# Small f32 matmuls on halves and quarters of the array in a woven single-core kernel

## The chip, the cores and the metric

One core of a Trainium2 chip runs the whole program. The metric is the device time of one execution in microseconds; the median of several runs is compared.

## The reference

Two blocks of a language model are applied to 256 tokens of 2048 columns, in f32. The first block has two layers. In each, one projection feeds four groups of eight heads of 64 columns: retention, hgrn2, mlstm and rwkv7. Their outputs are joined and projected, and a gated feed-forward part follows. The second block has two attentions. What matters here, cut:

```python
# retention, in chunks; mlstm has the same shape, with its own decay, and a denominator
scores = jnp.einsum('bhtd,bhsd->bhts', qc, kc) * intra
out = jnp.einsum('bhts,bhse->bhte', scores, vc) + ...
# rwkv7, token by token
state = (state * jnp.exp(lwt)[:, :, None, :]
         - jnp.einsum('bhvk,bhk->bhv', state, kkt)[..., None] * (at * kkt)[:, :, None, :]
         + vt[..., None] * kt[:, :, None, :])
y = jnp.einsum('bhvk,bhk->bhv', state, rt)
# second block, first attention: three branches per head (compressed, selected, window)
o = g[..., 0:1] * o_cmp + g[..., 1:2] * o_sel + g[..., 2:3] * o_win
```

## The kernel before

The program is a series of stages, each a block in which every engine has its own instruction list and waits for the others by semaphores. The large products are split into a high and a low part of the weights: SP loads slabs of weights into a ring of four, ACT writes the high part (line 183), DVE or POOL the low part (line 191), and PE multiplies both with two parts of the activations. Between the stages of the mixers this work is woven in: `Woven` cuts the next projection into pieces (a quarter of a pair of output tiles and of its rows), and `weave.pe(pe, step)` issues as many pieces as the shares for that step say (lines 510 to 512, three matmuls for each 128 rows: 12 matmuls in a piece of a 2048-row matrix, 9 in the w_out piece of 1536 rows). In these stages POOL writes the low part, and two slabs (eight pieces) fit beside each other.

The rwkv group works in chunks of 64 tokens. A chunk needs the inverse of a triangular matrix, and `rwkv_solve_stage` builds it from products of matrices. A pass j takes two heads (hh) and two tiles of 128 tokens (tt), four matrices x. Each is 128x128 with its two 64x64 chunk blocks on the diagonal, and zeros elsewhere. The pass has ten steps: step 1 multiplies keys (64 rows deep) into four masked matrices; steps 2 to 7 square, multiply and add them; steps 8 to 10 apply three of them to the right-hand sides z. Every step is a burst of matmuls on PE (lines 1803 and after, all through the helper `mats`), then an evacuation from PSUM by DVE (lines 1884 to 1909), which PE awaits. `RWKV_SHARES` puts two woven pieces behind step 1, one behind steps 2, 3, 5 and 6, none behind the others.

`rwkv_output_stage` computes, per pass, masked products (line 2007) and then for each head and token tile two value products and two state products (lines 2018 to 2022).

`retention_stage` and `mlstm_stage` go head by head: `decayed_product` (lines 1100, 1101; 64 rows deep), woven pieces (four and three), then for the head before `weighted_values` (lines 1109, 1110; its output has 64 columns of the array), in mlstm twice, the second time with ones. DVE weights the products between the two (lines 1192 and 1351).

`attention_stage` goes by units of two heads and one query tile, with one or two key tiles: scores (lines 2592, 2595), soft-max on DVE and ACT, transposes (2610, 2614), value products (2625), with 3, 2 and 1 woven pieces between them in the first attention.

On PE one f32 matmul of the program is two instructions in the trace.

Of the kernel before, what the change touches and what calls it, by code (L numbers as in the profile page):

```python
# [13 lines left out]
P = 128  # L14
# [729 lines left out]
def constants():  # L744
# [48 lines left out]
    c["low8"] = chunk & b8 & (u < s)  # L793
    c["up8"] = chunk & b8 & (u > s)
    c["low_off"] = chunk & ~b8 & (u < s)
    c["up_strict"] = chunk & (u > s)
# [300 lines left out]
def decayed_product(pe, m, h, k, q, out):  # L1097

    j, r = h // 2, slice(HD * (h % 2), HD * (h % 2) + HD)
    m.nc.tensor.matmul(out[:, 0:T], k[r, j, 0:P], q[r, j, :], start=True, stop=True)  # L1100
    return m.nc.tensor.matmul(out[:, T:T + P], k[r, j, P:T], q[r, j, P:T], start=True, stop=True)


def weighted_values(pe, m, h, v, w, out, first=True):

    r = slice(HD * (h % 2), HD * (h % 2) + HD)
    m.nc.tensor.matmul(out[r, 0:T], v(0), w[:, 0:T], start=first, stop=False)
    return m.nc.tensor.matmul(out[r, P:T], v(1), w[:, T:T + P], start=False, stop=True)  # L1110
# [10 lines left out]
def retention_stage(m, p, weave):  # L1121
# [13 lines left out]
    with nc.Block() as block:  # L1135
        @block.sync
        def _(sp):
            tables.start(sp, cs, m.const_dram("ret_cos_sin"))
            tables.start(sp, decay, m.const_dram("ret_decay").rearrange("p (h n) -> p h n", h=NH))
            weave.sp(sp, NH + 1)  # L1140

        @block.tensor
        def _(pe):
# [7 lines left out]
            for h in range(NH + 1):  # L1151
                if h < NH:
                    if h >= 2:

                        pe.wait_ge(*weights.at(h - 1))
                    decayed_product(pe, m, h, k, q, m.ps[:, 2 + h % 2, :]).then_inc(*scores.up())
                    weave.pe(pe, 1 + h)
                if h >= 1:
                    g_ = h - 1
                    pe.wait_ge(*weights.at(h))  # L1160
                    weighted_values(pe, m, g_, lambda st: vt[:, st, g_ * HD:(g_ + 1) * HD], pr[:, g_ % 2, :],
                                    m.ps[:, g_ // 4, (g_ // 2 % 2) * T:(g_ // 2 % 2) * T + T]).then_inc(*o_done.up())
            weave.pe(pe, NH + 1)

        @block.gpsimd
        def _(pool):
            weave.pool(pool, NH + 1)

        @block.scalar
        def _(act):  # L1170
# [3 lines left out]
            weave.act(act, NH)  # L1174
            act.wait_ge(*o_done.at(NH))
            nc.scalar.activation(q, m.banks(0, 2).rearrange("p (a b) -> p a b", b=T), ACT.Copy)
            weave.act(act, NH + 1)

        @block.vector
        def _(dve):  # L1180
# [7 lines left out]
            for h in range(NH):  # L1188
                dve.wait_ge(*scores.at(h + 1))
                if h >= 2:  # L1190
                    dve.wait_ge(*o_done.at(h - 1))
                nc.vector.tensor_tensor(pr[:, h % 2, :], m.ps[:, 2 + h % 2, 0:384], decay[:, h, :], ALU.mult)\
                    .then_inc(*weights.up())
# [10 lines left out]
def mlstm_stage(m, par, gates, weave):  # L1204
# [26 lines left out]
    with nc.Block() as block:  # L1231
        @block.sync
        def _(sp):
            moved.start(sp, log_f, m.tmp[NH:2 * NH, 1, 0, :])
            tables.start(sp, mask, m.const_dram("mlstm_mask"))
            weave.sp(sp, NH + 3)

        @block.tensor
        def _(pe):
# [24 lines left out]
            for h in range(NH + 1):  # L1264
                if h < NH:
                    if h >= 2:
                        pe.wait_ge(*weights.at(h - 1))
                    decayed_product(pe, m, h, k, q, m.ps[:, 4 + h % 2, :]).then_inc(*scores.up())
                    weave.pe(pe, 3 + h)
                if h >= 1:  # L1270
                    g = h - 1

                    pe.wait_ge(*weights.at(h))
                    half = (g // 2 % 2) * T
                    weighted_values(pe, m, g, lambda st: vt[:, st, g * HD:(g + 1) * HD], pr[:, g % 2, :],
                                    m.ps[:, g // 4, half:half + T])
                    weighted_values(pe, m, g, lambda st: ones[:, 0:HD], pr[:, g % 2, :],
                                    m.ps[:, 2 + g // 4, half:half + T]).then_inc(*o_done.up())
            weave.pe(pe, NH + 3)

        @block.gpsimd
        def _(pool):
            weave.pool(pool, NH + 3)

        @block.scalar
        def _(act):
# [13 lines left out]
            weave.act(act, NH + 2)  # L1300
            act.wait_ge(*o_done.at(NH))
            nc.scalar.activation(acc[:, 0:GT, :], m.banks(2, 2).rearrange("p (a b) -> p a b", b=T), ACT.Abs).then_inc(*den_ready.up())
            weave.act(act, NH + 3)

        @block.vector
        def _(dve):
# [40 lines left out]
            for h in range(NH):  # L1347
                dve.wait_ge(*scores.at(h + 1))
                if h >= 2:
                    dve.wait_ge(*o_done.at(h - 1))  # L1350
                nc.vector.tensor_tensor(pr[:, h % 2, :], m.ps[:, 4 + h % 2, 0:384], ex[:, h, :], ALU.mult)\
                    .then_inc(*weights.up())
            dve.wait_ge(*o_done.at(NH))
# [390 lines left out]
def mask4(ap):  # L1744

    return ap.unsqueeze(1).unsqueeze(1).broadcast_to([P, 2, 2, P])
# [5 lines left out]
def rwkv_solve_stage(m, weave):  # L1752
# [8 lines left out]
    masks = m.flat(S_AT, 6 * P).rearrange("p (a b) -> p a b", b=P)  # L1761
# [9 lines left out]
    x1 = m.tmp[:, 0, 2:4, :].rearrange("p a (x n) -> p (a x) n", n=P)  # L1771
# [9 lines left out]
    with nc.Block() as block:  # L1781
        @block.sync
        def _(sp):
            for n, name in enumerate(("low8", "up8", "low_off", "up_strict", "up_incl", "up_incl_neg")):
# [1133 lines left out]
```

## Time and profile before

| | |
|---|---|
| median of 3 runs | 4463.32 us |
| lowest, highest | 4458.55, 4469.31 us |
| the profiled execution | 4464.4 us, span 4462.1 us |
| mean granted TensorE clock | 0.934 |
| PE busy | 3881.6 us (87%) |
| DVE, ACT, POOL busy | 2094.1, 1695.6, 1647.4 us (47, 38, 37%) |

The page gives the busy time of every engine over the span; PE is a matmul engine whose ends are modelled, so that its busy time says little of its pace. The timeline lists instructions in order of time and merges equal ones that follow each other; the brackets give the idle time of the engine before them and what ended it. A granted clock of 1.00 is 2.4 GHz, 0.50 is 1.2 GHz.

### The profile page before, as it was taken

Reading aid. Unit: us, or ns where it says so; the run is one execution under the profiler, and the core shown is the slowest. Engines: PE = TensorE matmul, PEld = TensorE weight load, DVE = VectorE, ACT = ScalarE, POOL = GpSimd, SP = SyncE. Lnnn points to the kernel's source line nnn. Section 1 sums busy time; section 2 is a strip of 40 time slices with the busy share of each in tenths; the row PEclk is TensorE's granted clock in tenths of the full one; section 3 lists DMA queues with packets and bytes.
Section 4 is the critical chain, followed back from the end, with each engine's and each line's share of the span. In section 5 each row is a group of like instructions: output and inputs, shape, how many; then the busy total and the mean of one; then the engine's idle time right before and its main releaser. Section 6 shows DMA issues by size and latency. Waiting matters only on the chain. (4 is left out here: it accounts for less than half of the span.)

```text
span 4462.1 us, 58395 instructions
## 1 busy us (share of the span) xinstructions
PE 3881.6 (87%) x24692; PEld 3426.4 (77%) x24692; DVE 2094.1 (47%) x2118; ACT 1695.6 (38%) x1540; POOL 1647.4 (37%) x649
## 2 busy tenths in 40 slices
PE   6787888889999997887888979999996978989987
PEld 6676877778888886776777868888885877878776
DVE  4534543455454555633643255554455432344454
ACT  3402433344443443411543334444343324544433
POOL 0322555379992000321554449994000024440000
PEclk9898998999999998998899989999998979999998
DMA  4411333367775553411333447776552633335443
GB/s 159 132 48 55 102 122 116 130 201 232 237 237 166 184 184 126 136 52 43 104 106 116 165 137 239 238 241 197 160 180 95 203 111 98 114 107 180 162 149 113
DMA packets 379713, 655.58 MB, mean 147 GB/s; under 512 B 13792, under 2 KB 191856, under 8 KB 378384
## 3 DMA queue, kind: packets, MB, share of 16 engines
q1 hardware_dynamic: 364624, 598.50, 41.9%
q0 software_dynamic: 14912, 54.53, 3.6%
q8 instruction: 134, 2.20, 0.2%
q14 instruction: 43, 0.35, 0.0%
HBM read 645.63 MB, written 6.29 MB: 146 GB/s over the span
## 5 line engine op out<-in xcount | busy, mean ns | idle before, releaser
L212 PE MATMUL ps<-x_parts,w_hi 128*128 128x512 f32 x6160 | 2199.0, 401 | 172.5 <-ACTq L397 114.3
L213 PE MATMUL ps<-x_parts,w_lo 128*128 128x256 f32 x6160 | 1741.2, 283 | 0.0
L183 ACT ACTIVATE w_hi<-weight_ring 128x2048 fp32r<-128x2048 f32 (+1 forms) x564 | 1065.7, 1890 | 1723.7 <-PE ps L213 1125.0
L212 PEld LDWEIGHTS ps<-x_parts,w_hi 128*128 128x128 f32 x6160 | 1170.9, 190 | 470.9 <-issue 108.5
L191 DVE TENSOR_TENSOR w_lo<-weight_ring,w_hi 128x2048 fp32r<-128x2048 f32 x392 | 952.6, 2430 | 1113.8 <-ACT w_hi L183 1113.8
L191 POOL TENSOR_TENSOR w_lo<-weight_ring,w_hi 128x2048 fp32r<-128x2048 f32 (+1 forms) x172 | 790.3, 4598 | 1691.5 <-ACT w_hi L183 1691.5
L213 PEld LDWEIGHTS ps<-x_parts,w_lo 128*128 128x128 f32 x6160 | 1179.7, 192 | 0.0
L510 PE MATMUL ps<-x_parts,w_hi 128*128 128x256 f32 x2592 | 792.3, 306 | 130.4 <-POOL w_lo L191 67.2
L511 PE MATMUL ps<-x_parts,w_hi 128*128 128x256 f32 x2592 | 754.7, 291 | 0.0
L512 PE MATMUL ps<-x_parts,w_lo 128*128 128x256 f32 x2592 | 752.8, 290 | 0.0
L510 PEld LDWEIGHTS ps<-x_parts,w_hi 128*128 128x128 f32 x2592 | 518.7, 200 | 163.1 <-POOL w_lo L191 83.0
L511 PEld LDWEIGHTS ps<-x_parts,w_hi 128*128 128x128 f32 x2592 | 519.4, 200 | 3.9 <-issue 2.9
L512 PEld LDWEIGHTS ps<-x_parts,w_lo 128*128 128x128 f32 x2592 | 518.1, 200 | 0.0
L2310 POOL TENSOR_SCALAR spare<-spare,second_vectors 128x512 f32<-128x512 f32 x180 | 403.1, 2247 | 3.9
L2314 POOL TENSOR_TENSOR arena<-arena,spare 128x512 f32<-128x512 f32 x180 | 350.5, 1947 | 14.6
L1803 PE MATMUL ps<-arena 128*128 128x128 f32 (+2 forms) x1024 | 133.1, 297 | 38.5 <-DVE arena L1909 18.1
L113 POOL DMA_DIRECT2D arena<-in_w_ck x2 | 1.8, 909 | 436.8 <-DVE w_lo L191 436.8
L1803 PEld LDWEIGHTS ps<-arena 128*128 128x128 f32 (+1 forms) x1024 | 117.8, 205 | 51.4 <-DVE arena L1909 22.8
L113 POOL DMA_DIRECT2D spare<-in_w_ada x96 | 72.9, 759 | 178.2 <-POOLq L983 150.9
L1004 PE MATMUL ps<-arena,small_consts 128*128 128x256 f32 x256 | 76.7, 469 | 49.9 <-ACT arena L991 49.9
L1004 PEld LDWEIGHTS ps<-arena,small_consts 128*128 128x128 f32 x256 | 60.7, 242 | 65.6 <-ACT arena L991 54.4
L2683 DVE SCALAR_TENSOR_TENSOR arena<-ps,arena 128x256 f32<-128x256 f32 (+1 forms) x40 | 20.5, 553 | 176.8 <-PE ps L2595 139.9
(386 smaller groups left out, 2769.2 us busy)
## 6 DMA issues: line engine op xcount, KB each, us to landing
weight_ring<-in_w_in SPq DMA_DIRECT2D x212, 1024.0 KB, 5.2
weight_ring<-in_w_ffn_gate SPq DMA_DIRECT2D x88, 1024.0 KB, 5.3
weight_ring<-in_w_ffn_up SPq DMA_DIRECT2D x88, 1024.0 KB, 5.4
weight_ring<-in_w_ffn_down SPq DMA_DIRECT2D x88, 1024.0 KB, 5.6
spare<-in_w_ada POOLq DMA_DIRECT2D x96, 512.0 KB, 5.2
weight_ring<-in_w_out SPq DMA_DIRECT2D x32, 768.0 KB, 4.6
weight_ring<-in_w_out SPq DMA_DIRECT2D x24, 1024.0 KB, 5.1
weight_ring<-in_w_br_a SPq DMA_DIRECT2D x8, 1024.0 KB, 5.0
```

The lines of the kernel that those rows point to most:

```text
L113: eng.dma_start(dst, src).then_inc(self.rec[0], 16)
L183: core.nc.scalar.activation(core.w_hi[:, g % 2, at], core.ring[:, (self.start + g) % RING, at], ACT.Copy)\
L191: (ops or core.nc.vector).tensor_tensor(core.w_lo[:, g % 2, at], core.ring[:, (self.start + g) % RING, at], core.w_hi[:, g % 2, at].bitcas ...
L212: mm(out, hi, core.x_parts[:, x, :, :].rearrange("p a t -> p (a t)"), start=first, stop=False)
L213: return mm(out[:, 0:T], lo, core.x_hi[:, x, :], start=False, stop=last)
L510: mm(out, hi, x_hi, start=(kk == 0), stop=False)
L511: mm(out, hi, x_lo, start=False, stop=False)
L512: last = mm(out, lo, x_hi, start=False, stop=(kk == 2 * self.ks - 1))
L1004: mm = nc.tensor.matmul(m.ps[:, n, 0:T], m.const("ones"), sq[:, k, :], start=(k == 0), stop=(k == KT - 1))
L1803: return nc.tensor.matmul(at, lhs, right, start=True, stop=True)
L2310: ins = nc.gpsimd.tensor_scalar(to, buf[:, n % 2, k, :], c[:, 2 * s + k:2 * s + k + 1], None, ALU.mult)
L2314: done(pool, nc.gpsimd.tensor_tensor(out, out, buf[:, n % 2, k, :], ALU.add), step)
```

## The change

In the solve all chunk matrices are kept compact: 128 partitions (two chunks of 64) by 64 columns, four matrices in 256 columns of an array or a PSUM bank. A product of two of them is two matmuls of 64x64 on 64 columns, one in the quarter of rows and columns 0 to 63, one in that of 64 to 127. The masks are cut to 64 columns, and the unit matrix is the stacked one. Step 1 computes each chunk block by itself, in all four quarters. The right-hand sides keep their 512 columns. Retention and mlstm go by pairs of heads, whose matmuls alternate between the two row halves or column halves, and their woven pieces come in steps of 8 and 6. The output stage does the same, token tile by token tile. The first attention issues the value products alternately for its two column halves, and both attentions issue the scores in the order 0, 2, 1, 3.

```diff
-    c["low8"] = chunk & b8 & (u < s)
...
+        return np.take_along_axis(x, i[:, None] // CHUNK * CHUNK + np.arange(CHUNK)[None, :], 1)
+    c["low8"] = own_chunk(b8 & (u < s))
...
+def decayed_products(pe, m, j, k, q, bank):
+    for hh, r in by_halves():
+        m.nc.tensor.matmul(m.ps[:, bank + hh, 0:T], k[r, j, 0:P], q[r, j, :], start=True, stop=True)
+    for hh, r in by_halves():
+        mm = m.nc.tensor.matmul(m.ps[:, bank + hh, T:T + P], k[r, j, P:T], q[r, j, P:T], start=True, stop=True)
+    return mm
+def weighted_values(pe, m, v, w, out):
+    for hh, r in by_halves():
+        m.nc.tensor.matmul(out[r, 0:T], v(hh, 0), w[:, hh, 0:T], start=True, stop=False)
+    for hh, r in by_halves():
+        mm = m.nc.tensor.matmul(out[r, P:T], v(hh, 1), w[:, hh, T:T + P], start=False, stop=True)
+    return mm
...
+            for j in range(GT + 1):
+                if j < GT:
+                    if j:
+                        pe.wait_ge(*weights.at(2 * j))
+                    decayed_products(pe, m, j, k, q, 2).then_inc(*scores.up())
+                if j:
+                    n = j - 1
+                    pe.wait_ge(*weights.at(2 * j))
+                    weighted_values(pe, m, lambda hh, st: vt[:, st, (2 * n + hh) * HD:(2 * n + hh + 1) * HD], pr,
+                                    m.ps[:, n // 2, n % 2 * T:n % 2 * T + T]).then_inc(*o_done.up())
+                if j < GT:
+                    weave.pe(pe, 1 + j)
...
-        return m.flat(t0, 512).rearrange("p (x n) -> p x n", n=P)
+        return m.flat(t0, 4 * CHUNK).rearrange("p (x n) -> p x n", n=CHUNK)
...
-            def mats(bank, lhs, right, x, out=None):
-                at = m.ps[:, bank, x * P:(x + 1) * P] if out is None else out
-                return nc.tensor.matmul(at, lhs, right, start=True, stop=True)
+            def mats(out, lhs, right):
+                for r in chunk_rows():
+                    mm = nc.tensor.matmul(out[r], lhs[r], right[r], start=True, stop=True)
+                return mm
...
-                        for hh in range(2):
-                            r = slice(HD * hh, HD * hh + HD)
-                            mm = mats(0, l[r, j, tk], rr[r, j, tk], 2 * hh + tt, m.ps[:, bank + 3 * hh, tk])
+                        for hh, r in by_halves():
+                            for c, out_rows in enumerate(chunk_rows()):
+                                tk = slice(tt * P + c * CHUNK, tt * P + c * CHUNK + CHUNK)
+                                mm = nc.tensor.matmul(m.ps[out_rows, bank + 3 * hh, tt * CHUNK:(tt + 1) * CHUNK],
+                                                      l[r, j, tk], rr[r, j, tk], start=True, stop=True)
...
-            ps = [m.ps[:, b, :].rearrange("p (x n) -> p x n", n=P) for b in range(3)]
+            ps = [m.ps[:, b, 0:4 * CHUNK].rearrange("p (x n) -> p x n", n=CHUNK) for b in range(3)]
...
+                for tt in range(2):
+                    at = j % 2 * T + tt * P
...
+                    for hh in range(2):
+                        nc.tensor.matmul(outs[hh][:, at:at + P], vt[:, tt, heads[hh]], low[:, 0, 2 * hh + tt, :], start=True, stop=False)
...
-MLSTM_SHARES = ([6, 2, 7] + [3] * NH + [2], [2, 64])
-RETENTION_SHARES = ([8] + [4] * NH + [3], [3, 64])
+MLSTM_SHARES = ([6, 2, 7] + [6] * GT + [2], [2, 64])
+RETENTION_SHARES = ([8] + [8] * GT + [3], [3, 64])
...
-                for x, (q, keys, bank) in enumerate(items):
+                for x in (0, 2, 1, 3):
+                    q, keys, bank = items[x]
...
+                order = [(n, o) for n in range(size) for o in range(len(outs))] if cmp is not None else \
+                    [(n, o) for o in range(len(outs)) for n in range(size)]
```

Two places of PE's list show how the instructions move. The first is the start of a pass of the solve (L1803 is `mats` before; L1826 is `mats` and L1842 the products of step 1 after). Before:

```order
L1803 MATMUL ps<-arena 128x128 x4
L1803 MATMUL ps<-arena 128x2x64 x12
L1803 MATMUL ps<-arena 128x128 x12
L510 MATMUL ps<-x_parts,w_hi 128x256
L511 MATMUL ps<-x_parts,w_hi 128x256
L512 MATMUL ps<-x_parts,w_lo 128x256
```

After:

```order
L1826 MATMUL ps<-arena 64x64 x8
L1826 MATMUL ps<-arena 64x2x64 x24
L1842 MATMUL ps<-arena 64x64 x24
L510 MATMUL ps<-x_parts,w_hi 128x256
L511 MATMUL ps<-x_parts,w_hi 128x256
L512 MATMUL ps<-x_parts,w_lo 128x256
```

These rows are step 7 (four products), steps 8 to 10 (twelve) and step 1 of the next pass (twelve). Every product has become two, each on a quarter; what stands between them has not moved.

The second place is the mlstm stage, between two woven stretches. Before, the values and the ones of one head and the products of a later one:

```order
L1109 MATMUL ps<-arena 64x256
L1110 MATMUL ps<-arena 64x128
L1109 MATMUL ps<-arena,small_consts 64x256
L1110 MATMUL ps<-arena,small_consts 64x128
L1100 MATMUL ps<-arena 128x256
L1101 MATMUL ps<-arena 128x128
L510 MATMUL ps<-x_parts,w_hi 128x256
```

After, twice as many of each for a pair of heads, the products first (L1109 and L1111 are now `decayed_products`, L1118 and L1120 `weighted_values`):

```order
L1109 MATMUL ps<-arena 128x256 x2
L1111 MATMUL ps<-arena 128x128 x2
L1118 MATMUL ps<-arena 64x256 x2
L1120 MATMUL ps<-arena 64x128 x2
L1118 MATMUL ps<-arena,small_consts 64x256 x2
L1120 MATMUL ps<-arena,small_consts 64x128 x2
L510 MATMUL ps<-x_parts,w_hi 128x256
```

The bursts of two heads have come together, and the woven stretches between them have grown from three pieces to six.

## Rows read from the trace of the kernel before

**Rows 1.** The page: the weight splitting groups of part 5.

```profile
L183 ACT ACTIVATE w_hi<-weight_ring 128x2048 fp32r<-128x2048 f32 (+1 forms) x564 | 1065.7, 1890 | 1723.7 <-PE ps L213 1125.0
...
L191 POOL TENSOR_TENSOR w_lo<-weight_ring,w_hi 128x2048 fp32r<-128x2048 f32 (+1 forms) x172 | 790.3, 4598 | 1691.5 <-ACT w_hi L183 1691.5
```

**Rows 2.** Timeline of PE, solve, layer 0, first pass: start, length, what ran, [idle].

```profile
214.90 1.61 PE L1803 MATMUL ps<-arena 64*128 64x128 f32 x24
...
219.42 2.79 PE L1803 MATMUL ps<-arena 128*128 128x128 f32 x24
...
223.92 2.05 PE L1803 MATMUL ps<-arena 128*128 128x128 f32 x16 [0.23 <-DVE tmp L1892]
...
227.42 1.16 PE L1803 MATMUL ps<-tmp,arena 128*128 128x128 f32 x8
...
234.35 2.05 PE L1803 MATMUL ps<-arena 128*128 128x128 f32 x16 [0.55 <-DVE arena L1901]
...
239.86 1.16 PE L1803 MATMUL ps<-arena 128*128 128x128 f32 x8 [0.85 <-DVE arena L1906]
```

**Rows 3.** Timeline of DVE in the same pass.

```profile
216.65 2.48 DVE L1884 TENSOR_TENSOR arena<-ps,arena 128x512 f32<-128x512 f32 x4 [17.17 <-PE ps L1803]
...
223.45 0.42 DVE L1892 COPY tmp<-ps 128x256 f32<-128x256 f32 x1
...
228.68 0.69 DVE L1897 TENSOR_TENSOR arena<-tmp,ps 128x512 f32<-128x512 f32 x1 [1.32 <-PE ps L1803]
```

**Rows 4.** Windows: us; busy (x) of PE, PEld, DVE, ACT, POOL; PEclk; DMA; GB/s.

```profile
214.90:345.30 130.40, 110.15 (x865) 102.08 (x864) 51.58 (x84) 13.81 (x13) 27.22 (x6) 0.93 0.16 49
1911.45:2038.90 127.45, 107.49 (x865) 99.61 (x864) 51.62 (x84) 13.81 (x13) 27.22 (x6) 0.96 0.16 50
1984.44:2015.34 30.90, 25.91 (x218) 24.01 (x218) 12.90 (x21) 2.56 (x3) 8.43 (x2) 1.00 0.22 69
216.65:250.42 33.77, 28.77 (x217) 26.57 (x217) 12.91 (x21) 4.09 (x3) 9.07 (x2) 0.88 0.20 63
245.00:250.00 5.00, 4.15 (x32) 3.86 (x30) 0.69 (x1) 0.00 (x0) 0.00 (x0) 0.50 0.69 210
350.00:395.00 45.00, 39.87 (x408) 33.69 (x407) 13.65 (x24) 6.80 (x7) 9.03 (x2) 0.96 0.08 24
```

**Rows 5.** Timeline of PE, output stage, layer 0.

```profile
352.45 0.68 PE L1981 MATMUL ps<-arena 64*64 64x64 f32 x16
...
362.08 1.56 PE L1992 MATMUL ps<-arena,tmp 64*64 64x64 f32 x64
...
369.35 0.43 PE L2018 MATMUL ps<-arena 128*64 128x128 f32 x2
...
369.93 0.44 PE L2022 MATMUL ps<-arena 64*64 64x64 f32 x4
370.30 0.43 PE L2018 MATMUL ps<-arena 128*64 128x128 f32 x2
```

**Rows 6.** Timeline of PE, mlstm stage, layer 0.

```profile
633.30 0.65 PE L1109 MATMUL ps<-arena 128*64 128x256 f32 x2
...
634.00 0.59 PE L1109 MATMUL ps<-arena,small_consts 128*64 128x256 f32 x2
...
634.74 0.70 PE L1100 MATMUL ps<-arena 64*128 64x256 f32 x2
...
635.59 0.39 PE L510 MATMUL ps<-x_parts,w_hi 128*128 128x256 f32 x1
```

**Rows 7.** Timeline of PE, hgrn stage, layer 0.

```profile
484.35 0.87 PE L1453 MATMUL ps<-arena,h 128*64 128x256 f32 x8
```

**Rows 8.** Timeline of PE, first attention of the second block.

```profile
3709.93 0.72 PE L2592 MATMUL ps<-arena 64*128 64x128 f32 x8
...
3719.29 1.09 PE L2625 MATMUL ps<-arena 128*64 128x128 f32 x8
...
3722.04 0.39 PE L510 MATMUL ps<-x_parts,w_hi 128*128 128x256 f32 x1
```

More of the change, by code:

```diff
@@ L1094, in head_norm_stage, with by_halves @@
     m.end()
[L1097 to L1110, printed above, removed]
+def by_halves():
+    return [(hh, slice(HD * hh, HD * hh + HD)) for hh in range(2)]
+def decayed_products(pe, m, j, k, q, bank):
[10 more added lines that the diff above has]
+    return mm
 def transpose_values(pe, m, v, bank):
@@ L1150, in _ @@
             pe.wait_ge(*v_ready.at(1))
[L1151 to L1163, printed above, removed]
+            for j in range(GT + 1):
[10 more added lines that the diff above has]
+                    weave.pe(pe, 1 + j)
+            weave.pe(pe, GT + 1)
         @block.gpsimd
         def _(pool):
-            weave.pool(pool, NH + 1)
+            weave.pool(pool, GT + 1)
         @block.scalar
@@ L1187, in _ @@
             nc.vector.tensor_tensor(qk, qk, rot, ALU.add).then_inc(*qk_ready.up())
[L1188 to L1193, printed above, removed]
+            for j in range(GT):
+                dve.wait_ge(*scores.at(j + 1))
+                if j:
+                    dve.wait_ge(*o_done.at(j))
+                for hh in range(2):
+                    nc.vector.tensor_tensor(pr[:, hh, :], m.ps[:, 2 + hh, 0:384], decay[:, 2 * j + hh, :], ALU.mult)\
+                        .then_inc(*weights.up())
     m.end()
@@ L1346, in _ @@
             done(dve, nc.vector.tensor_tensor(ex, ex, bcast(mask, NH), ALU.mult), masked)
[L1347 to L1353, printed above, removed]
+            for j in range(GT):
+                dve.wait_ge(*scores.at(j + 1))
+                if j:
+                    dve.wait_ge(*o_done.at(j))
+                for hh in range(2):
+                    nc.vector.tensor_tensor(pr[:, hh, :], m.ps[:, 4 + hh, 0:384], ex[:, 2 * j + hh, :], ALU.mult)\
+                        .then_inc(*weights.up())
+            dve.wait_ge(*o_done.at(GT))
             dve.wait_ge(*least.at(1))
@@ L1744, in mask4, with chunk_rows @@
 def mask4(ap):
-    return ap.unsqueeze(1).unsqueeze(1).broadcast_to([P, 2, 2, P])
+    return ap.unsqueeze(1).unsqueeze(1).broadcast_to([P, 2, 2, ap.shape[-1]])
+def chunk_rows():
+    return [slice(CHUNK * c, CHUNK * c + CHUNK) for c in range(2)]
 SOLVE_STEPS = 1 + 10 * GT
@@ L1783, in _ @@
         def _(sp):
-            for n, name in enumerate(("low8", "up8", "low_off", "up_strict", "up_incl", "up_incl_neg")):
+            for n, name in enumerate(("low8", "up8", "low_off", "up_strict")):
                 tables.start(sp, masks[:, n, :], m.const_dram(name))
+            for n, name in enumerate(("up_incl", "up_incl_neg")):
+                tables.start(sp, incl[:, 4 + n, :], m.const_dram(name))
             weave.sp(sp, SOLVE_STEPS - 1)
```

126 lines of the change are left out of this document (65 added, 61 removed).

## The prediction

> **What bounds the kernel now.** I read the page first, then the timeline of PE and of DVE in each stage that the diff touches. The profiled execution took 4464.4 us, 1.1 us above the median of the runs, 4463.32; the sums below are made against 4464.4. PE is the engine to watch. Everywhere in the touched stages it alternates bursts of small f32 matmuls with woven pieces (12 matmuls of the next projection in a stage that weaves a 2048-row matrix), and it stands still only for evacuations.
>
> In the solve one pass over two heads is a chain of ten steps: a burst, DVE's evacuation, and a woven piece that covers the evacuation where there is one. From start to start the first pass has 4.52 us for step 1 (214.90 to 219.42), 4.50 for step 2, 3.50 for step 3, 6.93 for steps 4 and 5, 5.51 for steps 6 and 7 (of which 2.01 step 7, as step 4: a burst of 1.16 and 0.85 of idle time) [rows 2]. An undisturbed pass, at a granted clock of 1.00, takes 30.90 us [rows 4], so steps 8 to 10 take 5.94. A burst of 24 instructions (an f32 matmul is two instructions) lasts 2.79 us, one of 16 2.05, one of 8 1.16 [rows 2]. Where no piece covers it, the evacuation costs 0.85 us of PE's idle time [rows 2]: 0.10 until DVE starts, 0.69 for 512 columns (227.42 + 1.16 = 228.58, DVE at 228.68 [rows 3]), 0.06 back. The first pass of layer 0 took 33.77 us at a mean clock of 0.88: in its window of 245 to 250 the clock stood at 0.50, the 1.2 GHz level, after bursts of 8 with idle time between them. The two solve stages take 130.40 and 127.45 us at 0.93 and 0.96 [rows 4], 258 together, 10 more than 8 x 30.90.
>
> **The price of a small matmul.** This is the number that everything hangs on.
> - One quarter of the array, one after the other: 4 instructions of 64x64 on 64 columns, 0.44 us. Two diagonal quarters in turn: 16 instructions, 0.68 us [rows 5]. Four more pairs cost 0.24 us, so a pair is a slot of 0.06 us, and two quarters of different rows and columns do work at once. A burst of 8 slots is 0.68, 16 slots 1.16, 24 slots 1.64.
> - The 64 instructions of L1992 last 1.56 us [rows 5], 0.024 each, so at times more than two quarters run together. That is the cheap end (a 24-slot burst at 1.2 us). The dear end is one quarter at a time, 0.06 for each instruction, 2.8 us for the same burst.
> - I take the 0.06 per pair, since L1981 goes through the same two diagonal quarters as the new solve.
> - Two column halves in turn: the hgrn stage runs 8 instructions (4 on 256, 4 on 128 columns) in 0.87 us [rows 7], while 4 such instructions on one half take 0.70 from start to start [rows 6]. So the second half is nearly free.
>
> **The solve.** Step 1 becomes 48 instructions in four quarters. Twelve slots give 0.92 instead of 1.61, and what follows the burst (4.52 - 1.61 = 2.91) stays: 3.83. Step 3 (and 6, which has the same form, 5.51 - 2.01 = 3.50): 16 slots and 1.45 of woven piece beyond the burst (3.50 - 2.05), 2.61 each. Step 2: 1.64 + 1.45 = 3.09. The evacuations shrink from 512 to 256 columns, 0.42 for a single one [rows 3] and about 0.37 in a row, so the pieces of steps 2, 3 and 6 hide them whole; the 0.23 and 0.55 of idle time that stand there now [rows 2] go, which I left in the 1.45 for the entry into the burst. Steps 4 and 7 have no piece: 0.68 + 0.10 + 0.42 + 0.06 = 1.26. Step 5 is late on DVE, since its third copy keeps 512 columns: 1.64 + 0.10 + 0.37 + 0.37 + 0.69 + 0.06 = 3.23. Steps 8 to 10 keep their 512-column evacuation: 0.68 + 0.85 = 1.53 each, 4.59. The pass is 3.83 + 3.09 + 2.61 + 1.26 + 3.23 + 2.61 + 1.26 + 4.59 = 22.5 us, 8.4 less, 67 for the eight. The four mask products of step 1 (2.48 us on DVE now [rows 3], some 1.5 then) lie beside two woven pieces before and after: nothing. So do the smaller mask tables.
>
> Against it stands the clock. Steps 7 to 10 are now 4.6 of 8.0 us busy; they will be 2.7 of 5.9. I expect six of eight passes to fall to the 1.2 GHz level there, and each to pay 4.5 us, more than the 2.9 us (33.77 - 30.90) of the pass above, because the bursts that carried the recovery are shorter. That is 26 us where 10 are paid now: 16 lost. The solve gives **51 us**.
>
> **The output stage.** For each head and token tile PE now spends 0.95 us (369.35 to 370.30) [rows 5], all on its path; in future the two heads of a pair go through the same sequence on opposite halves. Two saved per pair of heads, 0.95 x 2 x 4 x 2 layers = **15 us**.
>
> **Mlstm and retention.** Per head: 0.70 for the values, 0.74 for the sums with ones, 0.85 for the products [rows 6], 2.29 in all, and 1.55 in retention, which has no ones. Pairs pay it once: 2.29 x 4 x 2 = 18.3 and 1.55 x 4 x 2 = 12.4. DVE's weighting is covered by 6 or 8 pieces instead of 3 or 4. What comes due is the supply. A slab of weights needs 1.89 us on ACT and 4.60 on POOL [rows 1] after its buffer comes free, some 6.8 us with the hand-overs, and its predecessor holds PE 5.8 us (four pieces of 1.45). Now each mlstm slab has a head's work between its pieces. With pairs two slabs per layer have none, and the one after each waits 1.0 us: 4 us off the 18.3. Retention's slabs have three quarters of the rows and its pair work falls on every second slab boundary, so they do not wait. **14 + 12 us**.
>
> **Attention.** The value products of a unit with both key tiles run 10 instructions on one half of the columns, then 10 on the other, 2.75 us (3719.29 to 3722.04) [rows 8]. Taken in turn they need half, 1.37 less; units with one key tile have 12 instructions in place of 20, 0.82 less. Eight of each: 17.5, of which I leave 1 to the supply: **16.5 us**. The new order of the scores is worth nothing: 8 instructions of 64 rows on 128 columns last 0.72 us [rows 8], where 24 of them in strict turn last 1.61 [rows 2]; (1.61 - 0.72) / 16 = 0.056 each, half of the 0.11 of a full-height one, and eight of those in a single file would need over 0.9. The two row halves already overlap across such a short distance.
>
> The sum is 51 + 15 + 14 + 12 + 16.5 = 109: 4464.4 - 109 = 4355, or **4354** on the median's scale.
>
> **The rule that speaks against the change.** In the solve the two diagonal quarters write one PSUM bank, each its own 64 partitions; L1981 and L1992 [rows 5] write a bank for each row half, and no row of this trace shows two row halves writing one bank at once. The Trainium skill ("TensorEngine Tiling (Array Packing)", Restrictions and Gotchas, Gotcha 1) says that different row tiles cannot access the same PSUM bank simultaneously. By that rule the time is rival A's.
>
> **The rivals.**
> - A, one bank, one quarter at a time. A pair costs 0.12 instead of 0.06. Each pass has 120 such slots (all but step 1), 7.0 us, 56 for eight; the output stage loses 4. PE stays busier, so the clock's extra 16 is not paid. 109 - 56 - 4 + 16 = 65: **4398**. For it: no row to the contrary. Against it: the partitions differ, and column halves write one bank together without loss [rows 7].
> - B, the supply takes over. POOL's 4.60 and ACT's 1.89 [rows 1] decide in mlstm, retention and attention, and the 43 us there come to nothing: 109 - 43 = 66, **4397**. Against it: POOL is idle 1691 us for ACT, and ACT waits for PE [rows 1], so in most places PE is the late one.
> - C, slower: the clock stays at the 1.2 GHz level through both solves and output stages, as it was in the window of 245 to 250 [rows 4]. The solves keep PE busy for 110 and 107 us, less the 67 saved, and an output stage for 40 [rows 4], less 8: 215 us in all. Doubled, less the 26 already counted, they cost 189: **4543**. It decides against the change from 109 us of extra low-clock cost. Against it: the clock came back within the stages each time, and their means are 0.93 and 0.96 [rows 4].
>
> **How the numbers follow.** My forecast 0.78, A 0.12, B 0.06, C 0.03, and 0.01 for gains and losses that cancel. Differences under 0.2% (9 us) are about what a measurement of this kernel can't tell from none. Faster by more: 0.96; within: 0.01; slower: 0.03. With quarters at the cheap end (18 us more), no fall of the clock at all (26 more) and no waits for supply (5) the time would be 4305; all three together are unlikely, so the range begins at 4318. It ends at 4402, above A and B.
>
> **What would show it.** Bursts of the solve at 1.6, 1.2 and 0.7 us (A: 2.8, 2.0, 1.1); passes of 22.5 us where the clock stays up and some 27 where it falls; the clock low at the end of six of eight passes; an output stage of 1.9 us per pair of heads instead of 3.8; one value and one product burst per pair in mlstm and retention; value products of 1.4 us in attention, scores unchanged at 0.72. I am wrong if diagonal pairs take 0.12 us, if "PE waits for POOL" grows by tens of us, or if the woven matmuls of the solve run mostly at the low clock.

## The result, and the profile after

The changed kernel takes 4352.91 us (median of 4 runs, 4351.05 to 4353.90), beside 4466.32 for the kernel before: a ratio of 0.9748, 95% interval 0.9731 to 0.9765. Its profiled execution took 4353.9 us, span 4351.6, mean clock 0.932; against the execution of before (4464.4) that is 110.5 us less, where 109 were forecast.

The page of the kernel after: busy time of PE, and of the groups that answer to [rows 1].

```profile
PE 3769.8 (87%) x25844; PEld 3333.2 (77%) x25844; DVE 2056.8 (47%) x2118; ACT 1695.3 (39%) x1540; POOL 1645.1 (38%) x649
...
L191 POOL TENSOR_TENSOR w_lo<-weight_ring,w_hi 128x2048 fp32r<-128x2048 f32 (+1 forms) x172 | 790.8, 4602 | 1581.7 <-ACT w_hi L183 1581.6
...
L510 PE MATMUL ps<-x_parts,w_hi 128*128 128x256 f32 x2592 | 790.3, 305 | 140.5 <-POOL w_lo L191 76.4
```

PE lost 112 us of busy time. POOL's split costs the same as before, 4.6 us a slab. The woven matmuls of L510 wait 76.4 us for low parts; before it was 67.2.

**The solve.** The timeline of PE in the first pass of layer 0, as in [rows 2]; the helper `mats` is now L1826, step 1 L1842:

```profile
214.23 0.93 PE L1842 MATMUL ps<-arena 64*64 64x64 f32 x48
...
218.15 1.61 PE L1826 MATMUL ps<-arena 64*64 64x64 f32 x48
...
221.33 1.15 PE L1826 MATMUL ps<-arena 64*64 64x64 f32 x32
...
224.03 0.68 PE L1826 MATMUL ps<-tmp,arena 64*64 64x64 f32 x16
...
225.31 0.45 PE L1826 MATMUL ps<-arena 64*64 64x64 f32 x8 [0.59 <-DVE arena L1925]
225.59 0.39 PE L1826 MATMUL ps<-tmp,arena 64*64 64x128 f32 x4
...
228.88 1.15 PE L1826 MATMUL ps<-arena 64*64 64x64 f32 x32
...
231.59 0.68 PE L1826 MATMUL ps<-arena 64*64 64x64 f32 x16
232.86 1.09 PE L1826 MATMUL ps<-arena 64*64 64x128 f32 x16 [0.59 <-DVE arena L1934]
...
236.69 1.09 PE L1826 MATMUL ps<-arena 64*64 64x128 f32 x16 [0.86 <-DVE arena L1937]
238.64 0.93 PE L1842 MATMUL ps<-arena 64*64 64x64 f32 x48 [0.86 <-DVE arena L1937]
```

From start to start the steps take 3.92, 3.18, 2.70, 1.28, 3.57, 2.71, 1.27, and 1.88, 1.95, 1.95 us (between 236.69 and 238.64 lies step 10). The bursts of 8, 16 and 24 slots last 0.68, 1.15 and 1.61 us. But steps 8 to 10 show 1.09 us bursts of the form 64x128, and step 5 runs the same form between its 64x64 instructions. DVE in the same pass, as in [rows 3]:

```profile
215.32 1.42 DVE L1912 TENSOR_TENSOR arena<-ps,arena 128x256 f32<-128x256 f32 x4 [15.68 <-PE ps L1842]
...
228.05 0.68 DVE L1929 COPY arena<-ps 128x512 f32<-128x512 f32 x1
...
232.38 0.42 DVE L1934 COPY arena<-ps 128x256 f32<-128x256 f32 x1 [1.48 <-PE ps L1826]
```

The windows that answer to [rows 4]: both solve stages, one pass, a stretch of steps 8 to 10, and the 30 us behind the first solve.

```profile
214.23:312.21 97.98, 82.88 (x1441) 74.45 (x1440) 35.62 (x84) 13.82 (x13) 27.30 (x6) 1.00 0.22 66
1862.43:1960.04 97.61, 82.88 (x1441) 74.45 (x1440) 35.62 (x84) 13.82 (x13) 27.28 (x6) 1.00 0.22 66
214.23:238.64 24.41, 20.72 (x361) 18.61 (x360) 8.91 (x21) 4.48 (x4) 9.08 (x2) 1.00 0.14 45
234.00:239.00 5.00, 2.54 (x55) 2.06 (x59) 2.06 (x3) 0.00 (x0) 4.19 (x1) 1.00 0.01 3
312.00:342.00 30.00, 25.48 (x380) 23.72 (x380) 11.64 (x23) 5.01 (x4) 8.05 (x2) 0.83 0.12 37
```

The stages take 97.98 and 97.61 us instead of 130.44 and 127.41 (from the first burst to the end of DVE's last instruction): 32.5 and 29.8 less, **62 us**. All four passes of each run at a clock of 1.00, also where PE is busy for 2.54 of 5 us. In layer 0 it falls right behind the stage (0.83 over the next 30 us); in layer 1 it stays at 1.00 there for another 6 us.

**Output stage, mlstm, attention**, the timelines that answer to [rows 5, 6, 8]:

```profile
339.09 0.44 PE L2045 MATMUL ps<-arena 128*64 128x128 f32 x4
...
340.06 0.44 PE L2045 MATMUL ps<-arena 128*64 128x128 f32 x4
...
341.02 1.16 PE L2035 MATMUL ps<-arena 64*128 64x128 f32 x16
```

One head pair and tile takes 0.97 us, so a pair of heads 1.93 instead of 3.8.

```profile
597.07 0.70 PE L1109 MATMUL ps<-arena 64*128 64x256 f32 x4
...
597.92 0.65 PE L1118 MATMUL ps<-arena 128*64 128x256 f32 x4
...
598.62 0.60 PE L1118 MATMUL ps<-arena,small_consts 128*64 128x256 f32 x4
...
599.37 0.39 PE L510 MATMUL ps<-x_parts,w_hi 128*128 128x256 f32 x1
```

Both heads of a pair go through products, values and sums in 2.30 us (597.07 to 599.37), as one head did before.

```profile
3612.39 1.09 PE L2661 MATMUL ps<-arena 128*64 128x128 f32 x16
...
3613.78 0.39 PE L510 MATMUL ps<-x_parts,w_hi 128*128 128x256 f32 x1
```

The value products of a unit with two key tiles take 1.39 us (3612.39 to 3613.78), not 2.75.

### The profile page after: what moved, and what is told of

Read it like the earlier page. It is cut to its first block and busy times, and to the rows that moved or that the text cites. A ratio compares the mean times of both kernels' runs of the same rounds, so it can differ in the third digit from the quotient of the medians.

```text
span 4351.6 us, 60687 instructions
## 1 busy us (share of the span) xinstructions
PE 3769.8 (87%) x25844; PEld 3333.2 (77%) x25844; DVE 2056.8 (47%) x2118; ACT 1695.3 (39%) x1540; POOL 1645.1 (38%) x649
## 5 line engine op out<-in xcount | busy, mean ns | idle before, releaser
L510 PE MATMUL ps<-x_parts,w_hi 128*128 128x256 f32 x2592 | 790.3, 305 | 140.5 <-POOL w_lo L191 76.4
L510 PEld LDWEIGHTS ps<-x_parts,w_hi 128*128 128x128 f32 x2592 | 518.3, 200 | 175.1 <-POOL w_lo L191 93.5
L311 ACT ACTIVATE tmp<-ps 128x1024 f32<-128x1024 f32 x86 | 85.1, 990 | 42.0 <-PE ps L213 42.0
L1826 PE MATMUL ps<-arena 64*64 64x64 f32 (+1 forms) x1664 | 76.0, 234 | 23.1 <-DVE arena L1937 13.2
```

The lines of the kernel that those rows point to most:

```text
L311: nc.scalar.activation(tmp, core.ps[:, CB * par:CB * par + n, T:2 * T], ACT.Copy).then_inc(core.cross_copied.sem, 1)
L510: mm(out, hi, x_hi, start=(kk == 0), stop=False)
L1826: mm = nc.tensor.matmul(out[r], lhs[r], right[r], start=True, stop=True)
```

## The experiments

### Each part put back by itself

Four kernels, each the changed one with one part as in the kernel before.

```diff
# u_solve: rwkv_solve_stage, mask4 and four mask tables
-            def mats(out, lhs, right):
-                for r in chunk_rows():
+            def mats(bank, lhs, right, x, out=None):
# u_output: the last loop of rwkv_output_stage
-                for tt in range(2):
-                    at = j % 2 * T + tt * P
+                for hh in range(2):
+                    r, cols = ...
+                    for tt in range(2):
# u_pairs: retention_stage, mlstm_stage and their shares
-MLSTM_SHARES = ([6, 2, 7] + [6] * GT + [2], [2, 64])
+MLSTM_SHARES = ([6, 2, 7] + [3] * NH + [2], [2, 64])
# u_attn: attention_stage
-                for x in (0, 2, 1, 3):
-                order = ...
```

> The changed kernel with the solve stage and its mask tables as they were (128x128 blocks), all else changed. The trace of the changed kernel puts 32 us of the gain into the first solve and 30 into the second, so 62 us more than the changed kernel, near 4415, with the clock falling in some passes. The prediction had 51: 4404. If the solve's gain were partly taken back by later stages (supply of weights), it would be less than 50.

> The changed kernel with the output stage's loop over heads and token tiles as it was (one half of the array at a time). From the trace 7.7 us per layer, as predicted: 15 us more than the changed kernel. Rival: what is lost here is waited for elsewhere (weights, mlstm's supply), under 8.

> The changed kernel with mlstm and retention head by head as before, and their shares of woven pieces. Trace: 15.6 and 13, 28 us more than the changed kernel; predicted 26. Rival B (the supply had been hidden and takes over): under 10.

> The changed kernel with the orders of the scores and of the value products in attention as before. Theory 1, from the trace: 5 to 7 us more than the changed kernel, not the 16.5 predicted, since waits for the low parts of the weights (4.3 us more), for DVE (2.0) and a lower clock (3 to 4) stand where PE became free. Theory 2, the clock windows of that one execution were chance: then over 9.

Ratios to the kernel before: 0.9883 (0.9860 to 0.9906), 0.9773 (0.9754 to 0.9792), 0.9828 (0.9808 to 0.9848), 0.9766 (0.9747 to 0.9785). Less the 0.9748 of the changed kernel, times 4466, the solve is worth 60 us, the output stage 11, mlstm and retention 36, attention 8, each give or take 12. The sum of 115 stands beside a whole gain of 113, with an error of some 24: nothing speaks for one part living off another, but a share of 20 us would not be seen this way. The traces are finer. The solve stages of u_solve:

```profile
214.69:345.17 130.48, 110.17 (x865) 102.11 (x864) 51.63 (x84) 13.81 (x13) 27.20 (x6) 0.93 0.16 49
1887.51:2011.10 123.59, 103.65 (x865) 96.11 (x864) 51.63 (x84) 13.81 (x13) 27.20 (x6) 1.00 0.17 52
```

The first has the clock's falls of the kernel before; the second has none and takes 123.59 us, four times the 30.90 of [rows 4]. So two falls cost 6.9 us there, and the new solve is worth 26 us a layer from its steps alone and up to 6.9 more from falls that are gone. For the output stage the timeline gives 49.5 and 49.6 us in u_output from the last subtraction of the solve to the last state product, against 41.2 to 42.0 in seven of the eight such stretches of the other four kernels (43.3 in the eighth, which has the low clock shown above): 8 a layer, 16 in all. For mlstm and retention, from the first product of mlstm to the solve of the next layer, it gives 1288.5 us in u_pairs and 1276.3 on average in the four others, and in layer 1, up to the first scores, 1359.4 and 1347.7: 24 in all. These stretches hold other stages too. From the first to the last instruction of their own, the two stages of both layers take 354.6 us before, 355.1 in u_pairs, and 322.5 to 324.1 in the four others: 31 to 33 less.

For attention the medians leave 8, give or take 12, and decide nothing; the windows tell more. They run from the first scores of the first attention to the last multiplication of its soft-max, so that the value products of the last two of its sixteen units lie behind them. In order: u_attn, the changed kernel, and u_output (which has the new order).

```profile
3570.40:3788.10 217.70, 198.05 (x1578) 179.28 (x1578) 67.19 (x206) 105.92 (x250) 95.86 (x21) 0.98 0.35 108
```

```profile
3579.50:3790.70 211.20, 184.92 (x1578) 170.40 (x1578) 68.89 (x207) 105.82 (x250) 95.97 (x21) 0.96 0.37 112
```

```profile
3593.80:3810.40 216.60, 190.39 (x1578) 176.16 (x1578) 68.95 (x206) 106.02 (x250) 95.86 (x21) 0.93 0.36 109
```

With the order of before this stretch takes 217.7 us here and 217.9 in the kernel before. With the new one it takes 211.2 (changed kernel), 211.0 (u_solve), 213.7 (u_pairs), 213.7 (f_shift, below) and 216.6 (u_output), at clocks of 0.96, 0.96, 0.94, 0.94 and 0.93. The whole stage, to its last instruction, takes 239.7 us before and 239.5 in u_attn, and in the same five 230.8, 230.6, 234.2, 234.2 and 237.2. The waits of PE (total, times, longest), in u_attn and in the changed kernel:

```profile
PE ps L510 <- POOL w_lo L191: 3.6, 4, 1.5
...
PE ps L2639 <- DVE arena L2745: 1.8, 10, 0.2
```

```profile
PE ps L510 <- POOL w_lo L191: 7.9, 6, 2.4
...
PE ps L2640 <- DVE arena L2752: 3.8, 10, 1.0
```

The value products themselves fell from 36.3 to 18.5 us of busy time in the stretch, in line with the costing. Theory 1 stands in these traces, with the addition that the share taken by the clock varies between these executions: of 17.5 us the whole stage keeps 2 to 9.

In the second attention only the order of the scores is new. The stage takes 50.4 us before and 50.6 in u_attn, at a clock of 0.97, but 53.8 at 0.90 in the changed kernel, and as long in u_solve, u_output and u_pairs. So there 3.4 us are lost. It is not the order by itself: h_rhs (below) has the new order too, and takes 50.1 us at 0.97.

### Quarters in turn or in runs

```diff
-                for r in chunk_rows():
-                    mm = nc.tensor.matmul(out[r], lhs[r], right[r], start=True, stop=True)
+                todo.append((out, lhs, right))
...
+            def go():
+                for r in chunk_rows():
+                    for out, lhs, right in todo:
+                        mm = nc.tensor.matmul(out[r], lhs[r], right[r], start=True, stop=True)
```

> Steps 2 to 10 of the solve issue all instructions of the first diagonal quarter and then all of the second, instead of in turn. Theory 1: two quarters only overlap over a short distance, so runs of 8 or more on one quarter go in single file; bursts of 16 take 1.1 us instead of 0.68, of 32 2.1 instead of 1.15, those with 128 columns 1.9 instead of 1.09; some 8 us per pass, a solve stage of 128 instead of 96 us, and the time near 4417. Theory 2: whatever is issued next to it, a quarter is free when its own work is done: no change.

4435.5 us in one execution, beside 4459.2 of before. PE in the first pass, bursts of 48, 32, 16 and 16 instructions:

```profile
221.12 2.83 PE L1833 MATMUL ps<-arena 64*64 64x64 f32 x48
...
225.50 1.90 PE L1833 MATMUL ps<-arena 64*64 64x64 f32 x32
...
228.96 0.96 PE L1833 MATMUL ps<-tmp,arena 64*64 64x64 f32 x16
...
240.60 1.58 PE L1833 MATMUL ps<-arena 64*64 64x128 f32 x16 [0.59 <-DVE arena L1942]
```

The stage took 133.4 us at a clock of 0.90 instead of 98. The bursts of 48 and 32 last 1.7 times as long, so theory 1 holds; the bursts of 16 gain some overlap where the quarter changes (0.96, not 1.1; 1.58, not 1.9). It is the turn-taking, not the smaller tiles, that makes compact blocks worth having: with the same instructions in runs, the solve is slower than with 128x128 blocks (133.4 against 123.6 to 130.5). What makes it slower is the clock, though: its first pass, at a clock of 1.00, takes 30.63 us (217.19 to 247.82), where a pass of 128x128 blocks takes 30.90 [rows 4]. The same run shows what rival A would have looked like, and that the changed kernel is not it.

### The second quantity of the right-hand sides

```diff
-                    mm = mats(item(m.ps[:, 2, :], x), t1[:, x, :], item(rhs, x))
+                    mm = mats(item(m.ps[:, 2, :], x)[:, 0, :], t1[:, x, :], item(rhs, x)[:, 0, :])
...
-                        mm = mats(item(m.ps[:, 0, :], x), l[:, x, :], item(z, x))
+                        mm = mats(item(m.ps[:, 0, :], x)[:, 0, :], l[:, x, :], item(z, x)[:, 0, :])
```

> Leaves out of the solve the second quantity of the right-hand sides in the products of steps 5 and 8 to 10 (64 columns instead of 128; DVE's copies keep their size). Theory: what my pass of 22.5 us missed is that these products have 128 columns, so their bursts fall from 1.09 to 0.68 us and the pass from 24.4 to 22.8; the two solve stages 13 us shorter in all. Rival: the 1.09 comes from the form of the output, which is scattered over the bank; then nothing changes. The clock may fall in some passes, as the burst share of steps 7 to 10 falls to 0.49.

4354.7 us in one execution of a kernel that leaves out half of the right-hand sides: nothing gained. The bursts of steps 9 and 10:

```profile
236.72 0.68 PE L1826 MATMUL ps<-arena 64*64 64x64 f32 x16 [0.79 <-DVE arena L1937]
238.26 0.68 PE L1826 MATMUL ps<-arena 64*64 64x64 f32 x16 [0.86 <-DVE arena L1937]
```

and the windows of the first solve and of the start of its second pass:

```profile
217.01:312.72 95.71, 80.60 (x1441) 73.69 (x1440) 35.61 (x84) 13.82 (x13) 27.31 (x6) 0.94 0.22 68
240.00:244.00 4.00, 4.00 (x63) 3.88 (x57) 2.04 (x6) 0.00 (x0) 0.58 (x1) 0.57 0.56 168
```

The bursts are 0.68 us, as the theory said, and a pass up to its end 22.8. Yet the stages take 95.71 and 97.46 us, not the 91.4 and 91.0 that the shorter bursts alone would make them: the clock now falls at the end of every pass (0.50 from 240.6, 264.5, 288.4 and 312.3 in layer 0). That gives back 10.8 of 13.2 us. The fourth fall of each layer comes as the stage ends (312.72), so six falls share the 10.8: 1.8 us each. The changed kernel has such a fall as well, from 312.8, just behind its first solve (312.21), and none between its passes.

### The clock and the idle time between bursts

```diff
                     dve.wait_ge(*products.at(n + 8 + q))
+                    cp(rhs, m.ps[:, 0, :])
```

> One more copy of 512 columns on DVE ahead of the evacuation in each of steps 8 to 10, so that PE stands idle 0.7 us longer in each. That alone is 2.1 us per pass, 8.4 per solve stage: 104.6 instead of 96.2. Theory 1: the clock stayed up in the changed kernel because the stretch with idle time between its bursts (steps 7 to 10) is 7 us long instead of 8, and not for its busy share, which is the same: with 9.2 us the clock falls to the 1.2 GHz level in most passes, as it did in some passes before, and each costs 3 us more: a stage of 112 to 117. Theory 2: what matters is whether the array is used in full by the bursts: no fall, 104.6.

4386.0 us in one execution. The burst of step 9, the first solve, and the end of its first pass:

```profile
236.08 1.09 PE L1826 MATMUL ps<-arena 64*64 64x128 f32 x16 [1.39 <-DVE arena L1938]
```

```profile
214.96:326.77 111.81, 89.92 (x1441) 81.02 (x1440) 42.77 (x96) 13.81 (x13) 27.29 (x6) 0.91 0.19 58
240.00:244.00 4.00, 2.55 (x56) 2.03 (x53) 1.63 (x4) 0.00 (x0) 0.00 (x0) 0.50 0.84 262
```

The idle time of PE grew by 0.60 us in each of three steps (1.39, 1.46 and 1.45 us instead of 0.79, 0.86 and 0.86), 7.2 in a stage. That alone makes 98.0 + 7.2 = 105.2; the stage takes 111.8. (The expectation counts a stage from DVE's first instruction, 1.8 us less; so counted it took 110.0.) The clock falls in every pass, in both layers, and each fall costs some 1.7 us (6.6 for four). Theory 2 is out; theory 1 has the sign, and not the size (3 us each). So in these executions, one of each kernel, the changed kernel stands close to an edge: with 0.41 us less of burst in four steps, or 0.6 us more of idle time in three, the clock falls each time.

### Finer woven pieces

```diff
+PARTS = 4
-        ... for part in range(2)]
+        ... for part in range(PARTS)]
-RWKV_SHARES = (..., [2] + [2, 1, 1, 0, 1, 1, 0, 0, 0, 0] * GT, [2, 1, 1, 2, 1, 1, 1, 1, 1], ...)
+RWKV_SHARES = (..., [2] + [1, 0.5, 0.5, 0.5, 1, 0.5, 0.5, 0.5, 0.5, 0.5] * GT, [2, 1, 1, 2, 1, 1, 1, 1, 1], ...)
```

> Woven pieces of 6 matmuls (0.73 us) instead of 12, and in the solve the same number of matmuls per pass, spread over all ten steps (2, 1, 1, 1, 2, 1, 1, 1, 1, 1 half pieces) instead of five. Steps 4, 7, 8, 9 and 10 leave PE idle for 0.6 to 0.86 us each, 3.7 in a pass; half pieces cover nearly all of that, while steps 2, 3 and 6 each show some 0.2 to 0.3 and step 1 some more, since four masked copies outlast one and a half pieces. I expect 2 us less per pass, solve stages of 88 us and a time near 4337. Rival: the supply of weights is not ready in the new places and the gain is under 5 us in all.

4350.8 us in one execution, and solves of 96.15 and 96.05 us. The first pass did take 21.96 us (217.56 to 239.52) instead of 24.4. In the second, PE waited 3.08 us for DVE in step 3, and behind that wait the clock stood at the low level from 248.0 to 251.4; the pass took 26.1 us. POOL and DVE there:

```profile
241.60 4.53 POOL L191 TENSOR_TENSOR w_lo<-weight_ring,w_hi 128x2048 fp32r<-128x2048 f32 x1 [10.04 <-ACT w_hi L183]
```

```profile
242.03 4.37 DVE L1918 SCALAR_TENSOR_TENSOR arena<-arena,small_consts 128x256 f32<-128x256 f32 x1
```

The subtraction `y = unit - adt` (0.42 us in every pass of the changed kernel) began while POOL was splitting a slab and ended 0.27 us after POOL. The Trainium skill ("SBUF — State Buffer", Who interferes with whom) says that a VectorE operation with two SBUF inputs and a GpSimd operation that reads SBUF exclude each other, and that the one that issues second is blocked until the first has finished. The trace agrees, with 4.37 us for 0.42. The next kernel moves POOL's work away from it: one piece more ahead of the first pass, and two fewer in the output stage (the expectation says one; the other goes to the stage behind).

```diff
-RWKV_SHARES = (..., [2] + [1, 0.5, ...] * GT, [2, 1, 1, 2, 1, 1, 1, 1, 1], ...)
+RWKV_SHARES = (..., [3] + [1, 0.5, ...] * GT, [2, 1, 1, 1, 1, 1, 1, 1, 0], ...)
```

> Half pieces spread over the ten steps, as in f_even, and one piece more ahead of the first pass (one less in the output stage), which moves every split of a slab on POOL some 4 us earlier. In f_even the single subtraction on DVE that has all operands in SBUF lasted 4.37 us instead of 0.42 when it started while POOL was splitting a slab, in four of eight passes. Theory 1: DVE is held until POOL's instruction ends; with the splits at 4, 19 and 13 us of a pair of passes and the subtraction at 1.5 none is hit, all eight last 0.42, a pass takes 22.0 us as the first of f_even did, a solve stage some 87 us, and the whole 17 us less than the changed kernel: near 4337. Theory 2: it was something else in those passes (the order of the copies, the length of a piece): the 4.37 stays and the time is that of f_even.

**4332.65 us** (median of 6), ratio 0.9704 (0.9680 to 0.9729): 20 us less than the changed kernel by the ratios, give or take 13, and the two solves alone are 20 us shorter in the traces. The subtraction's eight instructions (min, median, max in ns), and both solves:

```profile
L1918 DVE SCALAR_TENSOR_TENSOR arena<-arena,small_consts x8: 424/479/535, 218.5 to 1913.5; 128x256 f32<-128x256 f32 x8
```

```profile
215.92:303.73 87.81, 86.48 (x1441) 75.45 (x1440) 35.83 (x84) 13.44 (x12) 27.34 (x6) 1.00 0.23 69
1845.22:1932.90 87.68, 86.39 (x1441) 75.44 (x1440) 35.81 (x84) 13.44 (x12) 27.34 (x6) 1.00 0.22 70
```

Theory 1 holds: with the same pieces in the same number of steps, only their phase against POOL differs, and the stage is 8.3 us shorter. In four of the eight passes the subtraction still begins 0.24 us before POOL's split ends, and takes 0.53. The clock is at 1.00 throughout.

### The attention's supply

```diff
-ATTENTION_A_SHARES = ([8, 2, 1, 2], [0] * 4 + [1] * 12 + [2], [3, 2, 1] * 15 + [3, 2, 1, 128])
+ATTENTION_A_SHARES = ([8, 2, 1, 2], [0] * 4 + [1] * 12 + [3], [3, 2, 1] * 15 + [3, 2, 1, 128])
```

> The changed kernel with one woven piece more in the stage before the first attention, so that slabs end at the first piece behind the transposes instead of the first piece of a unit. Theory 1: 7.9 us of waits for the low parts and the falls of the clock behind them came from where a slab's boundary fell in the unit, with the high part queued on ACT behind the exponentials; now under 3 us of waits, no fall after the first 16 us, and an attention stage of 205 us or less instead of 211 to 217. Theory 2: POOL or ACT simply has too much to do for the faster units: the waits only move, 211 or more.

4354.92 us, ratio 0.9748 (0.9723 to 0.9773): no change, though one of 8 us would lie within the error. The stretch of the windows above, and the waits of PE that now lead it:

```profile
3580.00:3789.30 209.30, 184.86 (x1581) 172.86 (x1582) 82.95 (x206) 107.32 (x251) 96.42 (x21) 0.95 0.36 110
```

```profile
PE ps L2640 <- DVE arena L2752: 19.5, 7, 2.8
PE ps L2622 <- PEq L2506: 7.4, 1, 7.4
```

The waits for low parts did go, all of them. In their place PE waits 19.5 us for the soft-max, DVE being busy for 82.95 us with the work that took it 68.89. I had looked at PE's side of the boundary only; the splits now start under DVE's instructions of two SBUF operands. One of these, on 30 columns (L2738), took 1.35 us on average instead of 0.46, which is 14.2 us in its sixteen and all that DVE is busier. Neither theory had this.

Nor did they have the second wait. Counted to its last instruction the stage does gain: 224.7 us, 6.1 less than in the changed kernel. But the piece more in the stage before lets ACT and POOL begin on one more slab there (POOL from 3574.69 to 3579.18), and the first scores come only behind it: PE stands idle for 7.4 us, where it was 0.9. From the start of the stage before to that of attention it is 42.8 us instead of 34.9, of which 1.45 is the piece. What the one stage gained, its start took back. With both edits (f_both) the result is that of f_shift alone:

> Both edits of f_shift and a_phase. If they are independent, the sum of their gains over the changed kernel: 17 and 8, near 4328; if f_shift gains nothing, 4345.

4333.88 us, ratio 0.9698 (0.9672 to 0.9724). The last run takes most of POOL's work away. It leaves out the low parts of three quarters of each slab's columns during the first attention:

```diff
-        at = slice(0, self.slot)
+        at = slice(0, self.slot // self.thin)
...
+    beside_a.thin = 4
```

> In the first attention POOL computes the low parts of only a quarter of each slab's columns (the rest of the products there use stale low parts, so that part of the woven projection is not computed as it should be); about 1.2 us on POOL for each slab instead of 4.6. Theory 1: the value products did give 17 us, and the attention stage kept 1 to 7 of them because POOL's splits are late for PE, hold DVE's small instructions, and by both let the clock fall: now no wait for low parts, under 2 us of waits for the softmax, no fall of the clock after the first 16 us, and a stage of about 201 us (217.8 - 17). Theory 2: the shorter bursts alone let the clock fall: falls remain and the stage stays above 207.

4343.2 us in one execution. The first attention:

```profile
3589.10:3788.10 199.00, 183.49 (x1578) 170.46 (x1578) 64.32 (x207) 105.61 (x250) 26.95 (x21) 0.96 0.39 119
```

No wait for low parts is left, and 1.2 us of waits for the soft-max; this stretch takes 199.0 us, 18.7 less than with the order of before. Some 4 of the 18.7 are waits that the old order had as well (3.6 for the low parts and 1.8 for the soft-max, against 1.2); there is no run of the old order with as little work on POOL. Theory 1 holds for the waits and, with that taken off, for the size. Two falls of the clock remained (0.63 and 0.57 in windows of 4 us), so not all falls hang on those waits.

## Why the prediction was right, and where it was not

- **A pair of diagonal quarters in 0.06 us**: right. 0.68, 1.15 and 1.61 us stand beside 0.68, 1.16 and 1.64. Both quarters write one PSUM bank, so rival A and the rule behind it (the Trainium skill, "TensorEngine Tiling (Array Packing)", Gotcha 1) do not hold here, for these two quarters; this trace is the row to the contrary that was missing.
- **Steps 1 to 4, 6 and 7**: 3.92, 3.18, 2.70, 1.28, 2.71, 1.27, each within 0.1 of its term.
- **Steps 5 and 8 to 10**: wrong. "Steps 8 to 10 keep their 512-column evacuation: 0.68 + 0.85 = 1.53 each" priced the bursts at 64 columns. The right-hand sides hold two quantities, and each product has 128 columns. The bursts take 1.09 and the steps 1.88, 1.95 and 1.95; step 5 takes 3.57 instead of 3.23. The pass is 24.4 us, not 22.5: 15 us lost over eight, 12 of them in these four steps. I had read that the right-hand sides keep their 512 columns and used it for the evacuation alone. h_rhs shows the 0.68 when one quantity is left out.
- **The clock in the solve**: wrong in the other direction. I expected six of eight passes to fall at 4.5 us each, 26 us where 10 are paid; none fell. The two misses are one: the expectation was made for 0.68 us bursts, and with those (h_rhs) all eight passes do fall, but for 1.8 us each, well under half of what I took. The 1.09 us bursts keep the clock up. Together the solve gave 62 us, not 51.
- **The output stage**: 1.93 us per pair of heads, as costed, and 16 us against u_output. Between the two profiled executions the stage is only 12.4 us shorter, since layer 0 has the low clock behind the solve.
- **Mlstm and retention**: 2.30 us per pair, as costed. The wait for supply is there (76.4 - 67.2 = 9.2 us more behind POOL in the program, 4.3 of it in attention). In mlstm it grew by 3.1 us (8.6 to 9.6 and 8.6 to 10.7), where 4 were costed. The two stages themselves are 32 us shorter, where 26 was forecast; the longer stretches with the stages between give 24, and the medians 36, give or take 12.
- **Attention**: wrong. "17.5, of which I leave 1 to the supply" should have left 9 to 15. The products gave 17.8 us of busy time; 4.3 came back as waits for low parts, 2.0 as waits for the soft-max, and the rest is put down to a lower clock. The changed kernel's own execution keeps 9.0 in the first attention and loses 3.4 to the clock in the second: 5.5 of 16.5. Rival B was the right mechanism in this stage alone: a_thin gets 18.7 us once POOL is out of the way, some 4 of them from waits that were there before. The split of a slab was judged by its length against the slab's matmuls, not by where it starts: ACT writes the high part behind the unit's exponentials.
- **The scores' new order**: costed at nothing. L2622 has 16.3 us of busy time for the same 128 instructions that take 15.8 in u_attn. It was not tried alone; in the second attention, where it is all that changed, the stage is longer only where the clock is lower.
- **Rival C**: no sign of it in the solves; the mean clock stayed at 0.93. But it did not rise either. At mean clocks of 0.934 and 0.932 the low level takes some 590 us of each execution, an estimate from the two levels: the 27 us of it that left the solve stages stand elsewhere in the changed kernel.

That the sum came out within 2 us is luck. Between the two profiled executions the solve gave 11 us more than forecast and mlstm and retention 6 more, attention 11 less and the output stage 3 less. The mechanism was right, quarters and halves at work at once on the path of PE; the clock was misjudged both in the solve and in attention.

## What to carry to other kernels

Compact blocks pay on PE when the instructions of different quarters take turns; issued in runs they were worth nothing at the full clock (30.6 us a pass against 30.9), and the falls of the clock came on top. Read the column count off every operand, not off the evacuation. When a burst is shortened, ask next whether the clock stays up, where the supply's instruction starts, and which DVE instructions with two SBUF operands lie under it: here the phase of POOL's splits was worth more than the pieces' size. And judge an edit beyond the edges of its stage: the piece that a_phase moved was paid for at the boundary before it.

## What the runs showed of the hardware that I had not expected

- Two diagonal quarters write the same PSUM bank at the full pace of 0.06 us per pair.
- The granted clock fell to the 1.2 GHz level at the end of 8 of 8 passes with 0.68 us bursts. With 1.09 us bursts and the same idle time between them (the changed kernel) it fell in none, only once just behind a solve; with 0.6 us more idle time it fell again in all. That is one execution of each kernel. A fall cost 1.7 to 1.8 us there, 3.4 in the solve of 128x128 blocks.
- One DVE instruction of two SBUF operands took 4.37 us instead of 0.42 beside a split on POOL. Instructions of the same size that read PSUM kept their 0.41 beside one (changed kernel, at 220.49 and 222.93, under the split from 220.25 to 224.82).
